# Output projection of a hybrid encoder: conv and attention halves summed apart, both norms' factors applied at the residual add

## What is computed

```python
y_att = rmsnorm(window_attention(q, k, v, sink), att_out_g)     # 512 columns
y_conv = rmsnorm(short_conv(bg, cg, u, conv_w), conv_out_g)     # 512 columns
x = x + jnp.concatenate([y_att, y_conv], axis=-1) @ w_out       # (256,1024) @ (1024,1024)

def rmsnorm(x, g):
    y = xf * lax.rsqrt(jnp.mean(xf * xf, axis=-1, keepdims=True) + EPS)
    return y * g
```

## Time and profile before

| | |
|---|---|
| time before, median of 3 runs | 1363.96 us (1361.51 to 1366.25) |
| profiled execution, its own time | 1361.95 us |
| its span, first to last instruction | 1360.5 us |
| TensorE busy | 1297.9 us, 95% of the span |
| VectorE busy | 553.3 us |
| ScalarE busy | 442.7 us |
| mean granted TensorE clock | 0.981 |

### The profile page before, as it was taken

How to read it: one execution, slowest core, us unless ns; L and a number is a source line. 1 busy time by engine, 2 the same in 40 slices (tenths; PEclk the granted TensorE clock), 3 DMA queues, 4 the chain that set the end, 5 groups by cost and what they waited for, 6 DMA issues and landing times.

```text
span 1360.5 us, 20505 instructions
## 1 busy us (share of the span) xinstructions
PE 1297.9 (95%) x8957; PEld 811.9 (60%) x8957; DVE 553.3 (41%) x804; ACT 442.7 (33%) x658; POOL 10.8 (1%) x35
## 2 busy tenths in 40 slices
PE   7989999998988999899799999999999999999997
PEld 6777788877777666667666484733333354333343
DVE  5674455545585654646566474410000001200003
ACT  6554444436552553535346263300000000000001
POOL 3000000000000000000000000000000000000000
PEclk9989999999988999899899999999999999999999
DMA  9335555374102999999999999999999999999992
GB/s 333 118 124 185 186 187 186 121 247 145 41 1 89 409 409 390 408 361 395 407 385 407 383 408 402 402 409 409 408 409 396 381 363 347 391 379 404 406 398 82
DMA packets 129067, 418.75 MB, mean 308 GB/s; under 512 B 4248, under 2 KB 8384, under 8 KB 128976
## 3 DMA queue, kind: packets, MB, share of 16 engines
q1 hardware_dynamic: 127872, 416.30, 79.2%
q0 software_dynamic: 544, 1.12, 0.3%
q10 hardware_dynamic: 560, 0.01, 0.0%
HBM read 416.37 MB, written 1.05 MB: 307 GB/s over the span
## 4 chain that ended last, share of the span: by engine, by line
PE 87%; DVE 5%; DMA 3%; ACT 3%; issue 1%; ACTq 0%; SPq 0%; DVEq 0%
PE bank L2036 26%; PE bank L2107 14%; PE bank L1694 13%; PE bank L1695 13%; PE bank L1696 13%; DMA ring<-in_moe_w_down 3%; PE bank L1972 2%; PE bank L1966 2%; PE bank L2055 1%; ACT raw_d L776 1%; DVE lo L1083 1%; DVE mx L1172 1%; DVE raw_d L1169 1%; DVE w_lo L1513 1%; PE bank L1803 1%; PE bank L1744 1%
## 5 line engine op out<-in xcount | busy, mean ns | idle before, releaser
L1513 DVE TENSOR_TENSOR w_lo<-ring,w_hi 128x1024 fp32r<-128x1024 f32 x168 | 202.1, 1224 | 69.5 <-ACT w_hi L711 61.7
L2036 PE MATMUL bank<-ring,late_acts 128*32 128x256 f32 (+3 forms) x1936 | 215.8, 434 | 0.0
L711 ACT ACTIVATE w_hi<-ring 128x1024 fp32r<-128x1024 f32 x168 | 174.9, 1058 | 101.1 <-PE bank L1696 77.8
L1694 PE MATMUL bank<-hi,act_hi 128*128 128x512 f32 (+1 forms) x400 | 156.1, 390 | 12.6 <-DVE lo L1083 6.6
L2036 PEld LDWEIGHTS bank<-ring,late_acts 128*32 128x32 f32 (+1 forms) x1936 | 85.7, 120 | 121.6 <-issue 100.8
L2107 PE MATMUL bank<-ring,at_buf 128*32 128x256 f32 (+1 forms) x1408 | 157.1, 450 | 0.5 <-ACT at_buf L711 0.5
L1695 PE MATMUL bank<-lo,act_hi 128*128 128x512 f32 (+1 forms) x400 | 153.9, 385 | 0.0
L1696 PE MATMUL bank<-hi,act_lo 128*128 128x512 f32 (+1 forms) x400 | 153.8, 384 | 0.0
L711 ACT ACTIVATE at_buf<-bank 128x256 f32<-128x256 f32 (+2 forms) x40 | 18.0, 450 | 412.7 <-PE bank L2055 412.7
L1083 DVE TENSOR_TENSOR lo<-raw_gu,hi 128x1024 fp32r<-128x1024 f32 x96 | 112.4, 1221 | 25.7 <-ACT hi L711 25.0
L1535 DVE TENSOR_TENSOR silu_buf<-silu_buf,bank 128x512 f32<-128x512 f32 (+2 forms) x56 | 29.4, 536 | 225.5 <-PE bank L2036 192.2
(11 more groups left out here) (240 smaller groups left out, 1272.0 us busy)
## 6 DMA issues: line engine op xcount, KB each, us to landing
ring<-in_moe_w_up SPq DMA_DIRECT2D x50, 2048.0 KB, 15.5
ring<-in_moe_w_down SPq DMA_DIRECT2D x49, 2048.0 KB, 15.6
ring<-in_moe_w_gate SPq DMA_DIRECT2D x48, 2048.0 KB, 15.1
raw_gu<-in_w_in SPq DMA_DIRECT2D x7, 2048.0 KB, 13.1
ring_after<-in_moe_w_gate SPq DMA_DIRECT2D x7, 2048.0 KB, 15.8
ring_after<-in_moe_w_down SPq DMA_DIRECT2D x7, 2048.0 KB, 16.9
ring_after<-in_moe_w_up SPq DMA_DIRECT2D x6, 2048.0 KB, 16.8
raw_gu<-in_dense_w_gate SPq DMA_DIRECT2D x5, 2048.0 KB, 8.1
```

The source lines that it names most:

```text
L711: return nc.scalar.activation(out, in_, ACT.Copy, **kw)
L1513: v.tensor_tensor(w_lo[:, n % WP, :], flat(u)[:, q * 1024:(q + 1) * 1024], w_hi[:, n % WP, :], ALU.subtract).then_inc(w_lo_done, 1)
L1694: mm(out, ah, wh, start=start, stop=False, **kw)
L2036: ins = mm(bank[b][c * g.n:(c + 1) * g.n, 0:width], acts[STEPS[s][0]][:, k, g.col:g.col + g.n], by_rows(u, n)[:, kl, c * width:(c + 1) * w ...
```

## The change

The norm factor is one number per token, and the output projection mixes columns within a token, so it can be applied behind the projection. The changed kernel sums the conv half (k = 4 to 7) and the attention half (k = 0 to 3) in banks of their own, and multiplies each sum by its factor where it is added to x. Each output column block therefore takes four banks in place of two and four adds in place of two, now with a factor per token (`scalar_tensor_tensor`). The conv half is first in the projection. The two wide multiplies by the factors (L1257, L1264) are gone. The conv half's squares are summed over its four blocks on VectorE first (`tensor_reduce`, read with a stride of 256 floats), and TensorE then needs two matmuls with one column each, whose result lies by token, so that the square root and the reciprocal are of 128 x 2. A one-element square root (`table_warm`) brings the table load ahead of the squares and copies.

```diff
+OUT_ORDER = (2, 3, 0, 1)
...
+        OUT_BANKS = ((2, 4), (6, 0))
+        CMS = 6
+        ROUTE_X = (2, 3, 2, 3)
+        LOGIT_T = (4, 5)
+        LOGITS = (7, 0)
+        KEY, RANKS, GAIN = 6, 1, 5
...
@@ ScalarE, mixer
                 probT_copy(layer, 1)
+                nc.scalar.activation(table_warm[:, :], eps[:, :], ACT.Sqrt)
                 pieces(22, 24)
+                act.wait_ge(yc_done, layer + 1)
+                for k in range(CT):
+                    copy(act_hi[:, 4 + k, :], yc[:, k, :], scale=g_conv[:, layer, k:k + 1]).then_inc(mixhi_done, 1)
+                nc.scalar.activation(sq, yc, ACT.Square).then_inc(sq_done, 1)
                 for t in range(NT):
                     act.wait_ge(att_done, 2 * layer + t + 1)
                     nc.scalar.activation(prob[:, t * 512:(t + 1) * 512],
                                          att[:, t, :], ACT.Square,
                                          accum_out=ss_a[:, t:t + 1]).then_inc(attss_done, 1)
-                act.wait_ge(yc_done, layer + 1)
-                nc.scalar.activation(sq, yc, ACT.Square).then_inc(sq_done, 1)
-                act.wait_ge(attms_done, layer + 1)
-                nc.scalar.activation(std_a[:, :], ss_a[:, :], ACT.Sqrt).then_inc(attstd_done, 1)
...
                 act.wait_ge(attT_done, layer + 1)
                 for k in range(4):
                     copy(act_hi[:, k, :], bank[k // 2][:, (k % 2) * 256:(k % 2) * 256 + 256],
                          scale=g_att[:, layer, k:k + 1]).then_inc(mixhi_done, 1)
...
+                act.wait_ge(cms_done, layer + 1)
+                nc.scalar.activation(std_c[:, :], bank[CMS][:, 0:NT], ACT.Sqrt, bias=eps[:, 0:1],
+                                     scale=1.0 / CW).then_inc(cstd_done, 1)
                 pieces(24, 26)
@@ VectorE, mixer
+                for k in range(CT):
+                    dve.wait_ge(mixhi_done, 8 * layer + k + 1)
+                    v.scalar_tensor_tensor(out=act_lo[:, 4 + k, :], in0=yc[:, k, :], scalar=g_conv[:, layer, k:k + 1],
+                                           in1=act_hi[:, 4 + k, :], op0=ALU.mult, op1=ALU.subtract).then_inc(mixlo_done, 1)
                 attended(layer, 1)
...
+                dve.wait_ge(sq_done, layer + 1)
+                v.tensor_reduce(sq_sum, sq.rearrange("p k n -> p n k"), AX, ALU.add).then_inc(sq_summed, 1)
                 pieces(22, 24)
...
-                    ins = v.tensor_scalar(att[:, t, :], att[:, t, :], rstd_a[:, t:t + 1], None, ALU.mult)
...
-                link(v.reciprocal(rstd_c, std_c))
...
-                        v.tensor_tensor(yc, yc, rstd_c.unsqueeze(1).to_broadcast([P, CT, SEQ]), ALU.mult)\
...
+                def add_out(c, t, part, scale):
+                    xs = x[:, t, c * 512:(c + 1) * 512]
+                    return v.scalar_tensor_tensor(out=xs, in0=bank[OUT_BANKS[c][part] + t][:, :], scalar=scale[:, t:t + 1],
+                                                  in1=xs, op0=ALU.mult, op1=ALU.add)
...
                 for c, name in enumerate(("out0", "out1")):
+                    dve.wait_ge(piece_used, base + MIX_FIRST[name] + 2)
+                    for t in range(NT):
+                        add_out(c, t, 0, rstd_c).then_inc(conv_added, 1)
...
-                        v.tensor_tensor(xs, xs, bank[4 + 2 * c + t][:, :], ALU.add).then_inc(x_changed, 1)
+                        dve.wait_ge(conv_added, 4 * layer + 2 * c + t + 1)
+                        add_out(c, t, 1, rstd_a).then_inc(x_changed, 1)
@@ TensorE, mixer
                 values(layer, 1)
-                pe.wait_ge(sq_done, layer + 1)
-                for k in range(CT):
-                    ins = mm(bank[2][:, 0:SEQ], ones[:, :], sq[:, k, :], start=k == 0, stop=k == CT - 1)
-                ins.then_inc(cms_done, 1)
-                pe.wait_ge(attn_done, layer + 1)
+                out_pieces(layer, 0, 0, 1)
+                pe.wait_ge(att_done, 2 * (layer + 1))
                 for k in range(4):
                     for t in range(NT):
                         c = (k % 2) * 256 + t * P
                         ins = tr(bank[k // 2][:, c:c + P], att[:, t, k:AW:4], ident[:, :])
                 ins.then_inc(attT_done, 1)
-                mix_pieces(layer, "out0", (4, 5), 0, 4)
+                out_pieces(layer, 0, 1, 2)
...
+                pe.wait_ge(sq_summed, layer + 1)
+                for t in range(NT):
+                    ins = mm(bank[CMS][:, t:t + 1], sq_sum[:, t * P:(t + 1) * P], ones[:, 0:1], start=True, stop=True)
+                ins.then_inc(cms_done, 1)
+                out_pieces(layer, 0, 2, 4)
+                pe.wait_ge(cstd_done, layer + 1)
...
+            def out_pieces(layer, c, j0, j1):
+                for j in range(j0, j1):
+                    n = MIX_BASE[layer] + MIX_FIRST[f"out{c}"] + j
+                    r = n % RING
+                    pe.wait_ge(lo_done, n + 1)
+                    for i in range(2):
+                        k = 2 * OUT_ORDER[j] + i
+                        pe.wait_ge(mixlo_done, KT * layer + 2 * j + i + 1)
+                        cc = slice(i * 512, (i + 1) * 512)
+                        b = OUT_BANKS[c][0 if k >= 4 else 1]
+                        for t in range(NT):
+                            tt = slice(t * P, (t + 1) * P)
+                            ins = three(bank[b + t][:, :], act_hi[:, k, tt], act_lo[:, k, tt],
+                                        hi[:, r, cc], lo[:, r, cc], k % 4 == 0, k % 4 == 3)
+                    ins.then_inc(piece_used, 1)
```

More of the change, by code:

```diff
@@ L1253, in mixer @@
+                v.tensor_reduce(sq_sum, sq.rearrange("p k n -> p n k"), AX, ALU.add).then_inc(sq_summed, 1)
                 pieces(22, 24)
+                for k in range(4):
+                    dve.wait_ge(mixhi_done, 8 * layer + 4 + k // 2 * 2 + 2)
+                    v.scalar_tensor_tensor(out=act_lo[:, k, :], in0=bank[k // 2][:, (k % 2) * 256:(k % 2) * 256 + 256],
+                                           scalar=g_att[:, layer, k:k + 1], in1=act_hi[:, k, :],
+                                           op0=ALU.mult, op1=ALU.subtract).then_inc(mixlo_done, 1)
@@ L1254, in mixer @@
                 dve.wait_ge(attstd_done, layer + 1)
-                link(v.reciprocal(rstd_a[:, :], std_a[:, :]))
-                for t in range(NT):
-                    ins = v.tensor_scalar(att[:, t, :], att[:, t, :], rstd_a[:, t:t + 1], None, ALU.mult)
-                ins.then_inc(attn_done, 1)
+                v.reciprocal(rstd_a[:, :], std_a[:, :])
                 dve.wait_ge(cstd_done, layer + 1)
-                link(v.reciprocal(rstd_c, std_c))
-                for k in range(KT):
-                    if k == 4:
-                        v.tensor_tensor(yc, yc, rstd_c.unsqueeze(1).to_broadcast([P, CT, SEQ]), ALU.mult)\
[L1265 to L1273, removed]
@@ L1274, in mixer @@
-                pieces(24, 26)
+                v.reciprocal(rstd_c[:, :], std_c[:, :]).then_inc(rstds_done, 1)
+                pieces(24, 26)
+                def add_out(c, t, part, scale):
+                    xs = x[:, t, c * 512:(c + 1) * 512]
+                    return v.scalar_tensor_tensor(out=xs, in0=bank[OUT_BANKS[c][part] + t][:, :], scalar=scale[:, t:t + 1],
+                                                  in1=xs, op0=ALU.mult, op1=ALU.add)
+                dve.wait_ge(rstds_done, layer + 1)
@@ L1810, in mixer @@
                 ins.then_inc(attT_done, 1)
-                mix_pieces(layer, "out0", (4, 5), 0, 4)
+                out_pieces(layer, 0, 1, 2)
                 if layer == 0:
-                    mix_pieces(layer, "out1", (6, 7), 0, 4)
-                else:
-                    mix_pieces(layer, "out1", (6, 7), 0, 2)
+                    pe.wait_ge(pool_done, POOL_STEPS)
+                pe.wait_ge(sq_summed, layer + 1)
[4 more added lines that the diff above has]
+                pe.wait_ge(cstd_done, layer + 1)
+                if layer == 0:
+                    out_pieces(layer, 1, 0, 4)
+                else:
+                    out_pieces(layer, 1, 0, 2)
+                    pe.wait_ge(x_changed, 10)
                     tr(bank[GAIN][:, 0:KT], g_route[:, :], ident[0:KT, 0:KT]).then_inc(g_turned, 1)
@@ L1818, in mixer @@
                     route_turn(0, 1, 10)
-                    mix_pieces(layer, "out1", (6, 7), 2, 3)
+                    out_pieces(layer, 1, 2, 3)
                     pe.wait_ge(router_ready, 1)
@@ L1938, in route @@
                     route_logits(1, t).then_inc(logT_done, 1)
+                mm(bank[KEY][:, 0:NE], eights[:, :], down_part[:, :], start=True, stop=False)
                 for t in range(NT):
```

42 lines of the change are left out of this document (16 added, 26 removed).

## The result

The changed kernel takes 1340.82 us (median of 4 runs, 1339.44 to 1341.14), the kernel before beside it 1364.22 (4 runs, 1361.51 to 1366.25; three of them gave the 1363.96 of the table): a ratio of 0.9825, 95% interval 0.9807 to 0.9842. The profiled execution took 1340.69 us with a span of 1339.0.

What follows compares the result with a forecast made beforehand. TensorE, with 87% of the last-ending chain, was taken as the bound. Savings of 7.47 and 7.42 us by layer plus 0.05 gave 14.9, rounded to 15: 1349.0 us, range 1344.5 to 1355.5.

Steps and rivals of the forecast that it cites:

- When the projection can start: Layer 0, output projection: needing only the conv half's split, its first matmul moves from 96.26 to 87.06, 9.20 us.
- What goes between the pieces: Inside the projection: eight attention transposes (1.23 us) and two one-column matmuls (0.5) stand between weight pieces, 1.73 us in all.
- Is the attention half ready: At the projection's third piece, due at 94.3: attention remainders allow a matmul at 93.0, so nothing stalls.
- the two bounds: VectorE's new strided reduction of 1024 floats: between 1.2 and 2.1 us.
- the cover: Time by which the attention half is ready ahead of the projection's third piece: 1.2 us.
- The adds, the key, the table load: Adds cost 0.15 us in all, the expert key's matmul leaving the path gains 0.2, the table load takes 1.28.
- The clock: TensorE's granted clock: expected to be 1.00 through the mixer's end.
- the first rival: The clock falls anyway at the projection: 3 us lost per layer, 9 gained, 1355 us; chance 0.07.
- The front's sum: Both layers' mixers: 7.47 us saved in layer 0, 7.42 in layer 1, adds and key +0.05, together 14.9.
- Queues: DMA queues: none added; expert weights wait for the routing, so their stream starts earlier by what the front saves.
- the sum: Whole kernel: 14.9 us saved, rounded to 15; profiled execution 1361.95 becomes 1347.0, median 1349.0; forecast as worked out 0.80.

Runs made afterwards that it cites:

- three-load run: Changed kernel with an exponential and a square root more, each with a table load, behind the first in both layers: 1352.01 us, ratio 0.9913.

## Why the prediction was right about the front and wrong about the time

*When the projection can start.* Right: forecast 87.06, came at 86.97, and 0.46 behind the values where 0.43 was written. The squares, the copies and the remainders lie where the working put them.

*What goes between the pieces.* Right in kind, somewhat too dear: 1.73 us a layer were written. From its first matmul to its last the projection takes 23.13 us in place of 21.62 in layer 0 and 25.18 in place of 23.76 in layer 1, so 1.51 and 1.42. The 1.23 us of the transposes count an end that the next matmul overlaps: the next one starts 0.99 us after them in that row, and 0.87 here.

*Is the attention half ready.* Right that nothing waits. The reduction took 2.01 us, near the upper of the two bounds (1.2 and 2.1); the cover then is 0.6.

*The adds, the key, the table load.* The four conv adds cost no time on the path. The load was 1.28 with no drain, as the row said. The Trainium skill's 2.66 us per switch (ScalarE: Activation LUTs, section "What ACT_TABLE_LOAD costs") did not show in the changed kernel nor with three loads.

*The clock.* It stayed at 1.00, so the first rival did not come. The three-load run shows a pause that does bring it down: 3.5 us in place of 0.46.

*The front's sum.* Between the two profiled executions layer 0 gave 7.50 us (the values of layer 1 end at 386.48, against 393.98), and at the first expert load it was 14.94 in all, against 14.9. Other executions start the load between 417.83 and 419.44 with the changed order and between 434.38 and 435.74 with the old one, a mean difference of 16.3; so the front gave 15 to 16. That the pair came so near 14.9 is partly luck: the 0.5 us that the pieces saved were lost again behind the projections, and the clock moves the sum by 1 to 2 us from one execution to the next where no line is edited. From 120 to 160 us, in the dense part, it is 0.96 in this pair and 1.00 in the copies with 192 and 64 bytes; in the repeat of the kernel before, the first projection piece of layer 0 ran at the 1.2 GHz level and took 1.6 us more.

*The step that failed* is "*Queues.* No DMA is added", with its "the stream starts earlier by what the front saves", and so the sum: it has no term for the buffers' new place. I read the diff for instructions and waits, and two tiles of 8 bytes were neither. They moved the weight buffers from 192 past a multiple of 256 bytes to 0, the stream's top rate rose from 409 to 420 GB/s, and that gave 4 to 6 us more. The place is shown as the cause: 64 idle bytes in the kernel before give 5.6, and 64, 128 or 192 in the changed one take 3.9 to 5.3 back.

The place is not the whole of the 8 us that were missed. With the buffers at 192, 128 and 64 the changed kernel is 16.9, 18.3 and 18.2 us faster than the kernel before beside it, where 15 were forecast. Up to 1.3 of the 2 to 3 us left are the front, which gave 16.3 on average. The rest, 1 to 2 us, shows in the expert part and stays open: behind the first load these three take 924.2 us on average, the kernel before, also past a multiple of 256, 926.1 and 925.9.

## What to carry to other kernels

Read a diff for what it allocates as well as for what it executes. A new tile of a few bytes shifts every buffer behind it, and here a stream of weights at its limit felt whether its buffers start at a multiple of 256 bytes; in a kernel that streams, align those buffers on purpose and test a change at equal placement. A faster transfer helped here only where TensorE waited, which a stretch of the expert part shows at once: busy throughout, or not. And a wait costs more than its length where it is long enough to bring the clock down: two more table loads, 3.0 us of work a layer, cost 5.6 us in layer 0 and 4.9 in layer 1.

## What was not expected of the hardware

- The start of the weight buffers in SBUF set the stream's top rate: 420 GB/s at a multiple of 256 bytes, 408 to 409 at 64, 128 and 192 past it, with the same packets (127872 of them for 416.30 MB). That it is not graded is not explained by any run here.
- A reduction of 1024 floats that are read with a stride of 256 took 2008 to 2011 ns in the changed kernel; contiguous ones cost (686 - 161) / 504 = 1.04 ns a float, this one close to twice that.
